# Gate projections of a sparse-attention layer: the first two column chunks taken together over each token group

## The reference, cut to what matters

```
h     = rms_norm(x)                                  # 2048 x 1024
gates = silu(h @ w_in[:, gate_a]), silu(h @ w_in[:, gate_b])       # 512 + 512 columns
        sigmoid(h @ w_in[:, m_a] + b), sigmoid(h @ w_in[:, m_b] + b)   # 1024 + 1024 columns
score[q, s] = sum over 8 heads of w[q, head] * relu(q_idx[q, head] . k_idx[s])
sel[q]      = the 256 keys s <= q with the highest score    # becomes a mask for the sparse attention
```

## Time and profile before

| | us |
|---|---|
| median of 3 runs (3973.41 to 3980.95) | 3974.18 |
| profiled execution | 3973.37 |
| its span | 3971.6 |
| index stage, from the first load to the last mask tile | about 1203 to 1925 |
| gate matmuls (L80 to L82 of `i_p_g`), first to last | 1237.7 to 1907.1 |

### The profile page before, as it was taken

How to read it: one execution, slowest core, us unless ns; L and a number is a source line. 1 busy time by engine, 2 the same in 40 slices (tenths; PEclk the granted TensorE clock), 3 DMA queues, 4 the chain that set the end, 5 groups by cost and what they waited for, 6 DMA issues and landing times. The chain is left out here.

```text
span 3971.6 us, 50151 instructions
## 1 busy us (share of the span) xinstructions
PE 3265.2 (82%) x16836; PEld 2698.5 (68%) x16836; DVE 2086.2 (53%) x4934; ACT 1748.0 (44%) x3248; POOL 794.6 (20%) x927
## 2 busy tenths in 40 slices
PE   4897553899995989999489996879789997777689
PEld 3896443688884777777367775768678886566577
DVE  2201996788882555655399886331130000677643
ACT  2211653567673655666277773011131111666621
POOL 2200874011112322111021001112130000333221
PEclk9998676899997999999699998989899998888999
DMA  6612587434317222222521105545332223444364
GB/s 167 215 58 85 158 239 202 98 88 95 71 32 229 81 74 70 68 77 69 110 54 36 39 17 174 196 149 175 117 104 74 69 77 85 80 80 80 69 212 159
DMA packets 428596, 429.92 MB, mean 108 GB/s; under 512 B 73888, under 2 KB 341968, under 8 KB 424640
## 3 DMA queue, kind: packets, MB, share of 16 engines
q1 hardware_dynamic: 396464, 364.08, 33.1%
q0 software_dynamic: 8272, 29.69, 2.3%
q10 hardware_dynamic: 23616, 33.11, 2.3%
HBM read 251.28 MB, written 175.51 MB: 107 GB/s over the span
## 5 line engine op out<-in xcount | busy, mean ns | idle before, releaser
L355 ACT ACTIVATE p_ob<-p_ps 128x512 f32<-128x512 f32 (+2 forms) x164 | 81.5, 497 | 553.5 <-PE p_ps L82 552.5
L80 PE MATMUL i_p_g<-i_hT_lo,i_wh 128*128 128x512 f32 x768 | 312.2, 407 | 10.2 <-issue 7.0
L82 PE MATMUL i_p_g<-i_hT_hi,i_wh 128*128 128x512 f32 x768 | 307.8, 401 | 0.0
L81 PE MATMUL i_p_g<-i_hT_hi,i_wl 128*128 128x512 f32 x768 | 307.3, 400 | 0.0
L288 DVE CAST p_wh<-p_ws 128x1024 fp32r<-128x1024 f32 (+2 forms) x26 | 21.0, 807 | 499.0 <-PE p_ps L82 467.6
L1569 DVE SCALAR_TENSOR_TENSOR i_score<-i_relu,i_w,i_score 128x1024 f32<-128x1024 f32 (+7 forms) x154 | 156.3, 1024 | 200.6 <-ACT i_relu L1443 198.4
L80 PE MATMUL o_ps<-o_w_lo,o_ah 128*128 128x512 f32 x512 | 201.2, 393 | 40.9 <-DVE o_w_lo L2197 40.6
L80 PE MATMUL p_ps<-h2T_lo,p_wh 128*128 128x512 f32 x576 | 224.2, 389 | 2.3 <-DVE p_wl L290 2.3
L82 PE MATMUL p_ps<-h2T_hi,p_wh 128*128 128x512 f32 x576 | 224.1, 389 | 0.0
L81 PE MATMUL p_ps<-h2T_hi,p_wl 128*128 128x512 f32 x576 | 224.1, 389 | 0.0
L1454 ACT ACTIVATE i_above<-i_score,i_less 128x384 bf16<-128x384 f32 (+13 forms) x140 | 182.8, 1306 | 85.9 <-POOL i_less L1520 65.0
(11 more groups left out here) (316 smaller groups left out, 9400.4 us busy)
## 6 DMA issues: line engine op xcount, KB each, us to landing
scratch_gates<-i_ob SPq DMA_DIRECT2D x96, 256.0 KB, 2.1
m_m<-scratch_gates SPq DMA_DIRECT2D x64, 256.0 KB, 3.5
win_q_raw<-scratch_q2T SPq DMA_DIRECT2D x32, 512.0 KB, 7.6
scratch_qkT<-b_th SPq DMA_DIRECT2D x64, 192.0 KB, 3.4
scratch_qkT<-b_tl SPq DMA_DIRECT2D x64, 192.0 KB, 3.4
i_ws<-in_w_in SPq DMA_DIRECT2D x24, 512.0 KB, 4.4
p_ws<-in_a_w_in SPq DMA_DIRECT2D x18, 512.0 KB, 3.8
scratch_tm<-p_ob ACTq DMA_DIRECT2D x64, 137.0 KB, 1.8
```

The lines of the kernel that those rows point to most:

```text
L80: pe.matmul(out, l[0], r[1], start=start, stop=False)
L81: pe.matmul(out, l[1], r[0], start=False, stop=False)
L82: return pe.matmul(out, l[0], r[0], start=False, stop=stop)
```

## The change

The first 8 units alternate between chunk 0 and chunk 1, so that each token group is used twice in a row (group 0 by units 0 and 1, group 1 by units 2 and 3, and so on). From unit 8 on the order is as before. Two more things move with it. The load of chunk 2 is issued ahead of the first store. And W of chunk n >= 2 is now placed right behind the last step of the unit that frees its buffer (unit 4n - 5 for n >= 4), where it stood one unit later.

```
+def gate_step(u):
+    return (u % 2, u // 2) if u < 2 * NG else divmod(u, NG)
+def gate_done(chunk):
+    return 2 * NG - 1 + chunk if chunk < 2 else NG * (chunk + 1)
...
+    freed = {gate_done(n - 2) - 1: n for n in range(2, len(gate_chunks()))}
...
-            if k == KD - 1 and step % NG == 0:
-                n = step // NG + 1
-                if 2 <= n < len(gate_chunks()):
-                    steps.append(("W", n))
+            if k == KD - 1 and step in freed:
+                steps.append(("W", freed[step]))
...
-                n, g = divmod(u, NG)
-                if g == 0 and 1 <= n < len(wanted) - 1:
+                n, g = gate_step(u)
+                if u == 0:
+                    load(2)
+                elif g == 0 and 2 <= n < len(wanted) - 1:
                     load(n + 1)
...
-                    chunk, g = divmod(u, NG)
+                    chunk, g = gate_step(u)
...
-                        act.wait_ge(filled, NG * (chunk - 1))
+                        act.wait_ge(filled, gate_done(chunk - 2))
```

More of the change, by code:

```diff
@@ L1464, in _ @@
                     u = step[1]
-                    _, _, func, bias_col = wanted[u // NG]
+                    _, _, func, bias_col = wanted[gate_step(u)[0]]
                     act.wait_ge(filled, u + 1)
```

## The result

The changed kernel takes 4025.83 us (median of 4 runs, 4024.40 to 4028.99) against 3976.29 us for the kernel before, run beside it (4 runs, 3973.41 to 3980.95). The ratio is 1.0125, with a 95% interval from 1.011 to 1.014: some 50 us slower. The profiled execution took 4024.40 us.

What follows compares the result with a forecast made beforehand. TensorE was taken to bound the stage and so the program's end. Terms 35 + 4 + 8 + 8 - 4 = 51 us on 3973.4 gave 4024, as median 4025; range 4000 to 4055, 8 in 10 within 3988 to 4068.

Steps and rivals of the forecast that it cites:

- The mechanism: Rounding of chunks 3 to 23: ScalarE stands still 4.66 us for each load, 98 us over 21 loads.
- The opening: First units: TensorE's waits for token groups go; gain between 0 and 14.7 us, taken as 4.
- The earlier load of chunk 2: Issued behind the last input transfer and ahead of one store, where SyncE stands idle; cost nothing.
- Chunks 3 to 9: Short tiles, ScalarE nearly in lockstep with TensorE: stops cost 0.2 to 5.8 us, taken as 7 x 5 = 35 us.
- The replays: Stops traced through the old timeline: TensorE loses 5.8 us at chunk 4 and 5.5 us at chunk 9.
- Chunk 20: Stop ahead of M and T, as at chunk 4, in a late tile with some slack: 4 us.
- The other thirteen: Chunks 10, 12, 16, 18 (long waits for T) and 23 cost 0; 11, 13, 14, 15, 17, 19, 21, 22 cost 1 us each, 8.
- The replay of chunk 13: Longer rows, a scored piece every 3 to 4 us: TensorE's score waits 0.2 us for the delayed relu.
- The clock: TensorE at half rate for some 4 us behind each of about eight long new waits: 0 to 16 us, taken as 8.
- The range: Whole kernel, the forecast's own range: 4000 to 4055 us, chunks 3 to 9 between 2 and 5.8 us each, opening and clock at either end.
- All absorbed: Rival: every stop falls on ScalarE's slack or long waits for T, only the opening's gain remains; 3967 us, chance 16%.
- All paid: Rival: all stops but chunks 10, 12, 16, 18 and 23 reach TensorE, 88 plus 16 for the clock; 4078 us, chance 12%.

Runs made afterwards that it cites:

- the late rounding: The changed kernel with the rounding (W) of chunks 3 to 23 put back one unit later, opening and chunk 2 kept as changed: 3971.77 us, ratio 0.9993.
- the experiment: The changed kernel with only chunks 3 to 9 rounded early and chunks 10 to 23 rounded in the old place: 4002.4 us, ratio 1.0069.
- early loads: The changed kernel, rounding still early, with SyncE issuing each chunk's weight load three units earlier (chunk 3 one unit): 3981.34 us, ratio 1.0019.

## Why the prediction was right, point by point

**The mechanism.** Right. SyncE issues the load behind the store of the unit whose evacuation now stands directly ahead of the rounding, and ScalarE stops 21 times, 4.8 us each (4.66 predicted, 101.2 us against 98). Putting W back gives everything back; putting W early alone costs as much as the whole change.

**The opening, -4.** Right with the late rounding, within what can be measured: -3.0 us at unit 6, -3.6 at unit 95, -2.8 by the ratio. In the changed kernel itself it is -3.2 us at unit 7 and nothing of it shows at the end, against the kernel with early rounding and the old opening. The next thing late was the relu behind GpSimd's pause, as replayed: TensorE waits 6.33 us for it.

**The earlier load of chunk 2, nothing.** It was moved ahead of four stores, not one, and "SyncE stands idle there" was wrong. Its issue takes 6.70 us behind the token groups, and ScalarE's evacuation of unit 2 waits 3.66 us for a store, where it had waited 1.17. That this costs the end nothing was right in the one pair that varied it, though there the delay moved on to the query tiles. The first row shows SyncE of the changed kernel:

```profile
1250.82 6.70 SPq L1387 DMA_DIRECT2D i_ws<-in_w_in  x1
1271.70 0.60 ACT L1482 ACTIVATE i_ob<-i_p_g 128x512 f32<-128x512 f32 x1 [3.66 <-DMA scratch_gates<-i_ob]
```

**Chunks 3 to 9, 35 us.** Too large by 12, though the total looks right. From unit 7 to unit 35 the changed kernel takes 36.7 us longer, and the experiment gives 30. But the term was for waits alone, and the clock had a term of its own. The two stretches from unit 7 to 35 and from 35 to 95, first of the kernel before, then of the changed one:

```profile
1309.91:1499.44 189.53, 175.02 (x757) 140.92 (x756) 108.38 (x231) 117.06 (x194) 58.46 (x136) 0.97 0.26 78
1499.44:1907.52 408.08, 382.45 (x1621) 310.54 (x1619) 231.32 (x366) 247.87 (x306) 68.08 (x179) 0.96 0.23 70
```

```profile
1306.67:1532.92 226.25, 189.14 (x758) 150.56 (x757) 109.09 (x231) 118.28 (x194) 54.22 (x136) 0.90 0.21 65
1532.92:1960.86 427.94, 388.68 (x1621) 312.23 (x1619) 230.48 (x366) 245.88 (x306) 72.83 (x179) 0.95 0.22 67
```

TensorE's idle time grows by 37.1 - 14.5 = 22.6 us in the first, and its busy time for the same work by 14.1. The replays themselves were good: in the units behind the stops of chunks 4 and 9 idle time grows by 5.8 and 5.2 us (5.8 and 5.5 predicted). But these are the two dearest of the seven. The others have 4.0, 2.1, -1.6, 3.8 and 3.4 us, and the prediction gave each 5. With the lower clock the seven cost 4.4, 6.1, 4.9, -1.3, 5.9, 6.7 and 10.0 us by the evacuations. Two were not foreseen. At chunk 6 the stop costs nothing. GpSimd's pause, for which ScalarE had waited 5.7 us there, now passes while ScalarE stands still for the load, and 1.08 us of it is left:

```profile
1402.53 1.06 ACT L1474 ACTIVATE i_wh<-i_ws 128x1024 fp32r<-128x1024 f32 x1 [4.61 <-DMA i_ws<-in_w_in]
1408.01 1.04 ACT L1466 ACTIVATE i_above<-i_score,i_less 128x896 bf16<-128x896 f32 x1 [1.08 <-POOL i_less L1532]
```

At chunk 9 it is the other way round. The stop comes ahead of the pause (a wait of 5.82 us for GpSimd at 1516.49 follows), and TensorE waits two times and runs at the lower clock behind each. Tile 4's transposition waited 6.28 us (5.8 predicted).

**Chunk 20, 4 us.** Right: the transposition waits 4.26 us and the unit falls 4.5 us behind.

**The other thirteen, 8 us.** Somewhat low. With chunk 20 they were charged 12 us, and behind unit 35 idle time grows by 39.3 - 25.6 = 13.6 us, busy time by 6.2. By the evacuations, clock included, the four behind the long waits for T cost 3.0 us together (3.3 of it at chunk 12), and the last, nothing; the other eight 12.4, of it 8.7 at chunks 13 and 14. The replay of chunk 13 had found 0.2 us, and the trace has 3.4.

**The clock, 8 us.** Mis-sized. The term was the count of long waits times the half rate behind them, "about eight new waits". TensorE has 14 new waits for relus alone, and its busy time for the same work is 19.8 us longer (19.4 against the late rounding). The terms for waits were too large by nearly as much: 35 + 4 + 8 = 47 us was charged, and from unit 7 to 95 idle time grew by 22.6 + 13.6 = 36.2 us, while busy time grew by 20.4 where 8 was charged. The two errors cancel: 47 + 8 = 55, against 36.2 + 20.4 = 56.6. That the total is within 1 us of the median is partly luck. That TensorE's idle time is short behind the opening misread the kernel before as well: it had 12 waits for relus there, 40.3 us in all and up to 6.6 us.

**The range, 4000 to 4055.** The measured time lies inside. But the ends that the prediction names for it (2 and 5.8 us for each of chunks 3 to 9, the opening and the clock at either end) add up to about 3985 and 4043.

**The rivals.** *All absorbed* falls: ScalarE's slack did take 55 us (the three rows of waits above), over half of what was added, yet the stage is 53 us longer. *All paid* falls with chunks 10 to 23, 1.1 us each.

The Trainium skill (Perfetto Trace Analysis, Identifying the Most-Contended Engine) picks the engine by occupancy. It picked TensorE rightly, but TensorE lost its time to an engine that is busy for 55% of the stage (396.4 of 723.4 us), whose busy time did not change. The share tells whose time counts, not who takes it. The Trainium skill (DMA: Bandwidth & Descriptors, SWDGE vs HWDGE vs iDMA) also says that plain transfers belong on SyncE or ScalarE. The runs agree: some 11 and 19 us by moving the query tiles to SyncE, beside late and beside early loads.

## What to carry to other kernels

When a consumer is moved earlier on an in-order engine, move the issue of its load with it, and look what that load is ordered behind; here the store of the very unit that the consumer had moved up to. Price a stop by place: replay where the engine is in lockstep and where a longer wait lies behind the stop, since the same 4.7 us cost between -1 and 10 us. Replay more places than those that look dear before taking a mean. Keep clock and waits apart in the sum: take the idle time from the replays, and do not price the clock as small beside it. Here longer busy time at the lower clock was more than half as much as the new idle time (20.4 against 36.2 us).

## What was not expected of the hardware

- GpSimd's idle time behind its issue of loads grew where a 512 KB load of SyncE was under way at the same time: 5.90 us against 3.14 in one tile, 6.41 against 4.17 in another (early loads against the kernel before, and against the late rounding). It is not the only thing that lengthens it: in the changed kernel one of 5.13 us ends at 1624.23 with no such load under way. Which resource the two share was not tried.
- An issue on SyncE can last long: 0.43 us as a rule for the load of `i_ws`, 6.70 us behind the transfers of the token groups.
- Waits of TensorE as short as 2.41 and 2.75 us were followed by matmuls at the lower clock. Others of like length were not: behind 3.33 us at 1314.41 and 2.66 us at 1791.83 in the changed kernel the matmuls still take 0.39 us. So a wait's length alone did not tell whether the clock would fall.
